# Four granules of layer 0's modulation moved from VectorE's dot products to TensorE

## The chip, the core and the metric

The kernel runs on one core of a Trainium2 chip. The metric is the device time of one execution in microseconds (us). Before the change three runs took 1684.3, 1690.0 and 1689.28 us; their median is 1689.28 us.

## What is computed

A backbone of two layers over 512 tokens (256 context, stream 0, and 256 latent, stream 1), width 1024, float32. Each layer scales, shifts and gates with six vectors per stream that come from a condition vector:

```
mod_l[0..5] = split(silu(c)     @ w_ada[l] + b_ada[l])      # latent stream
mod_c[0..5] = split(silu(c_ctx) @ w_ada[l] + b_ada[l])      # context stream
h = rmsnorm(x, g1) * (1 + mod[1]) + mod[0];  x += mod[2] * mix_heads(h)
h = rmsnorm(x, g2) * (1 + mod[4]) + mod[3];  x += mod[5] * channel_mix(h)
```

`channel_mix` is a dense SwiGLU of width 2816 in layer 0 and a top-2-of-8 expert SwiGLU in layer 1. `w_ada[l]` is 1024 x 6144. The last sixth of its columns, which the change is about, makes mod[5], the gate of the channel mixing. It is first needed when the first down product of the dense SwiGLU is added to x.

## The kernel before

All of x, transposed, stays in SBUF as XT (eight tiles of 128 features x 512 tokens, k = 0 to 7). Weights stream in as granules of 128 x 2048 values (1 MB) through `raw`, a ring of three buffers (five at first); the order of the granules is written out by `stream_plan`, and the sync engine (SP) issues their loads in that order, each as soon as the granule that was in the buffer before has been used. A float32 product is made of three products of rounded parts: ScalarE casts a granule to w_hi (L1127, `upto`), VectorE makes w_lo as the difference (L1633), and TensorE computes hi x hi, hi x lo and lo x hi (`split3`, L448 to L450).

The modulation of layer 0 is made from 24 granules in two ways. Granules 0 to 19 (pairs n = 0 to 9) are `ada` granules: `group` multiplies the padded condition `cpad` (32 columns) with the raw granule on TensorE in plain float32 (L458), two granules for 512 outputs; ScalarE copies the result to `rows` (`save_row`, L1146), TensorE turns it (`turn`, L478: four products with a 128 x 2 result) and VectorE adds the bias into `mod` (`bias_mod`, L1691). Granules 20 to 23 are `dot` granules: VectorE computes each of two halves times two streams as one dot product of 1024 values (`dots`, L1646, and L1653 for the bias), with the condition in `crow`, which the POOL queue loads and ScalarE puts through silu (L1455). The same way is used for layer 1's 24 granules, in later steps of the dense SwiGLU.

The second norm of layer 0 goes as follows. `project_out` makes eight products o 0 to o 7; VectorE adds each to XT (L1999), ScalarE squares it (L1202), VectorE sums the squares (L1745). TensorE sums over partitions (`norm_sum`, L542), ScalarE takes the root (L1210), VectorE the inverse and four diagonal tiles (L1754, L1757), and TensorE spreads them (`norm_spread`, L551). Then VectorE computes t (L1770), ScalarE hT_hi (L1221) and VectorE hT_lo (L1779), for each k and each stream.

`feed_forward` runs over 33 steps, each with one granule: gate/up (two for each of 11 pairs) and down. On TensorE the first gate_up covers steps 0 and 1 together: it takes its granules and four PSUM banks, and then loops over k, waiting for hT_lo of tile k each time. A gate/up step uses banks 0 and 1, or 2 and 3; a down step makes eight products in banks 4, 5 and 6 by turns, and VectorE adds each to XT with the gate of mod (`add_gated`, L1999). Between them ScalarE applies silu (L1465) and casts (L1470), and VectorE multiplies (L2056, `h`) and makes the low part (L2059).

A PSUM bank is given out by `bank(job, b)`: TensorE waits until the last job in that bank has been read, by the count of the reading engine's instruction that is named "read ...". Each engine counts its instructions in its own order, so a wait for a name is a wait for everything that the engine has in front of it. The banks around the second norm are: o 0 0 to o 0 7 in 5, 7, 0, 1, 2, 3, 4, 5; the norm's sums in 6, its spread in 7; the first gate_up in 0, 1, 2, 3.

Of the kernel before, what the change touches and what calls it, by code (L numbers as in the profile page):

```python
# [21 lines left out]
P = 128  # L22
D = 1024
# [60 lines left out]
def dots_ahead():  # L84

    ahead = {2: [(0, 20), (0, 21)], 3: [(0, 22)], 4: [(0, 23)]}
    for i, b in enumerate((5, 7, 8, 10, 11, 13, 14, 16)):
        ahead[b] = [(1, i)]
    for i, b in enumerate((17, 19, 20, 22, 23, 25)):
        ahead[b] = [(1, 8 + 2 * i), (1, 9 + 2 * i)]  # L90
    for i, b in enumerate((26, 28, 29, 31)):
        ahead[b] = [(1, 20 + i)]
    return ahead


def stream_plan():

    plan = [("ada", 0, i) for i in range(2 * BEFORE - 2)]
    for l in range(DEPTH):
# [11 lines left out]
        if l == 0:  # L111
            before = dots_ahead()
            for b in range(3 * FC):
                plan += [("dot",) + x for x in before.get(b, [])]
                plan.append(("ffn", 0, b))
    return plan

# [19 lines left out]
def build(nc, io, table):  # L137
    with ExitStack() as ctx:
# [251 lines left out]
        def source(kind, e, i):  # L390
            if kind == "dot":
                return io["dot"][4 * e + i - (0 if e else 20)]
            return io[kind][e, i]
# [31 lines left out]
        def _(eng):  # L425
# [37 lines left out]
            def plain_group(n, half):  # L463

                if half == 0:
                    eng.wait_ge(act_done, after("cpad"))
                    state["plain"] = bank(f"ada 0 {n}", {9: 6}.get(n))
                group(0, n, half, state["plain"])
# [5 lines left out]
            def turn(l, n):  # L474
                eng.wait_ge(act_done, after(f"row {l} {n}"))
                o = bank(f"modT {l} {n}", 7 if n == 8 else None)
                for j in range(4):
# [350 lines left out]
            def feed_forward():  # L828
# [33 lines left out]
                for b, (kind, s, half) in enumerate(order):  # L862
                    if kind == "gu" and b != 1:
                        gate_up(b, 2 * s + half)
                    elif kind == "d":
                        down(b, s)
# [199 lines left out]
            for l in range(DEPTH):  # L1066
# [14 lines left out]
                attention(l, streams)  # L1081
                project_out(l, streams)
                norm_sum(l, 2, streams)
                if l == 0:
                    norm_spread(l, 2, streams)
                    feed_forward()
                else:
# [23 lines left out]
        def _(eng):  # L1111
# [338 lines left out]
            def feed_forward():  # L1450
                for b, (kind, s, half) in enumerate(order):
                    if b == 0:
                        upto(gindex[("ffn", 0, 1, 0)])
                        eng.wait_ge(*loaded["wide condition"])
# [112 lines left out]
            for l in range(DEPTH):  # L1567
# [18 lines left out]
                deviation(l, 2, streams)  # L1586
                if l == 0:
                    norm(l, 2, streams)
                    feed_forward()
# [27 lines left out]
        def _(eng):  # L1617
# [19 lines left out]
            def dots(g):  # L1637
# [3 lines left out]
                eng.wait_ge(raw_full[place[g]], 16 * use[g])  # L1641
                streams = (0, 1) if l == 0 or i < 8 else (1,)
                for j in range(2):
# [402 lines left out]

            def feed_forward():
                for b, (kind, s, half) in enumerate(order):
                    g = gindex[("ffn", 0, b, 0)]
                    upto(ahead(g, 2 if kind == "gu" else 1))  # L2050
                    if kind == "gu":
# [10 lines left out]
                    else:  # L2062
                        if s == 0:
                            eng.wait_ge(dve_done, after("dots 0 23"))
                        for k in range(KD):
# [419 lines left out]
def lay(inputs):  # L2485
# [6 lines left out]
    io["crow"] = c(np.broadcast_to(np.stack([f("c_ctx"), f("c")[0]]), (P, 2, D)))  # L2492
    io["ada"] = c(f("w_ada")[:1, :, :5120].reshape(1, 2, 4, P, 10, 512).transpose(0, 4, 1, 3, 2, 5).reshape(1, 20, P, GRAN))
    dot = f("w_ada").transpose(0, 2, 1).reshape(DEPTH * 24, 2, P, D).transpose(0, 2, 1, 3).reshape(DEPTH * 24, P, GRAN)
    io["dot"] = c(dot[20:])
    w_in = f("w_in")
# [122 lines left out]
```

## Time and profile before

| | |
|---|---|
| median of three runs | 1689.28 us |
| profiled execution, first to last instruction (span) | 1686.8 us |
| TensorE matmuls busy | 1611.4 us (96%) |
| VectorE busy | 1289.9 us (76%) |
| ScalarE busy | 897.8 us (53%) |
| mean granted TensorE clock | 0.982 of full |

Of the profiled execution only the span is given; the median of the runs stands 2.5 us above it. A busy TensorE is what the kernel is made of: the dense layer (about 317 to 697 us) and the experts (from some 870 us) keep it busy nearly without a break. So the places to read are those where it stands still, and who releases it there. In the rows below a time line gives for each instruction its start, its length, engine and line, operation, result and operands, and in square brackets how long the engine was idle before it and who ended that.

### The profile page before, as it was taken

The page shows a single profiled execution, that of the slowest core. Times are in us where ns is not written, and L with a number is a line of the kernel's source. Part 1 is how long each engine was busy: PE and PEld are TensorE (multiplying, and loading weights), DVE is VectorE, ACT ScalarE, POOL GpSimd, SP SyncE. Part 2 cuts the span into 40 slices and gives each one's busy share as a digit, 9 for nine tenths or more (in the row PEclk, how much of TensorE's full clock was granted, in tenths as well). Part 3 has the DMA queues.
Part 4 walks back from the last instruction along what each step waited for, and adds up shares of the span by engine and source line. Part 5 has one row for each costly group of instructions (what it writes and reads, how often), then busy time and mean ns, then how long its engine had stood idle before and what let it go on. Part 6 is the DMA issues. An engine that isn't in the chain of part 4 may idle for free.

```text
span 1686.8 us, 19520 instructions
## 1 busy us (share of the span) xinstructions
PE 1611.4 (96%) x7452; PEld 1269.6 (75%) x7452; DVE 1289.9 (76%) x1723; ACT 897.8 (53%) x1029; POOL 40.7 (2%) x40
## 2 busy tenths in 40 slices
PE   5999999899999999999899999999999999999996
PEld 2785567778888888786587778888888888888875
DVE  3944473698777865765768998898988889898997
ACT  3324363332222222444657777767777776777764
POOL 1000000000000000000000000000000000000050
PEclk8999999899999999999989999999999999999999
DMA  9225511363455544232147999899989999899982
GB/s 392 86 75 196 222 54 45 131 228 130 170 193 207 203 171 150 74 122 94 43 175 302 361 361 337 348 359 353 359 349 357 346 359 352 342 350 374 366 318 114
DMA packets 55972, 403.43 MB, mean 239 GB/s; under 512 B 6417, under 2 KB 6449, under 8 KB 8769
## 3 DMA queue, kind: packets, MB, share of 16 engines
q1 hardware_dynamic: 53712, 387.47, 60.3%
q0 software_dynamic: 2160, 14.63, 2.3%
q8 instruction: 62, 1.02, 0.2%
q14 instruction: 38, 0.30, 0.1%
HBM read 401.03 MB, written 1.05 MB: 238 GB/s over the span
## 4 chain that ended last, share of the span: by engine, by line
PE 74%; DVE 16%; ACT 5%; issue 3%; DMA 2%; SPq 0%; DVEq 0%; ACTq 0%
PE PS L448 20%; PE PS L450 20%; PE PS L449 20%; DVE w_lo L2272 6%; PE PS L753 2%; DVE w_lo L1633 2%; DMA arena<-in_ada 2%; ACT w_hi L1505 1%; DVE arena L1646 1%; PE PS L1008 1%; DVE XT L1999 1%; PE PS L765 1%; PE PS L778 1%; PE PS L732 1%; PE PS L458 1%
## 5 line engine op out<-in xcount | busy, mean ns | idle before, releaser
L2272 DVE TENSOR_TENSOR w_lo<-arena,w_hi 128x2048 fp32r<-128x2048 f32 (+1 forms) x136 | 305.9, 2254 | 43.3 <-ACT w_hi L1505 43.3
L2272 DVE TENSOR_TENSOR w_lo<-raw,w_hi 128x2048 fp32r<-128x2048 f32 (+1 forms) x133 | 298.9, 2251 | 32.9 <-ACT w_hi L1505 32.4
L1505 ACT CAST w_hi<-arena 128x2048 fp32r<-128x2048 f32 x132 | 251.5, 1909 | 46.2 <-PE PS L450 46.2
L1505 ACT CAST w_hi<-raw 128x2048 fp32r<-128x2048 f32 x129 | 246.9, 1916 | 43.5 <-PE PS L450 43.5
L448 PE MATMUL PS<-hT_hi,w_hi 128*128 128x512 f32 (+1 forms) x576 | 216.1, 375 | 8.6 <-DVE hT_lo L1779 6.9
L449 PE MATMUL PS<-hT_lo,w_hi 128*128 128x512 f32 (+1 forms) x576 | 213.7, 371 | 0.0
L450 PE MATMUL PS<-hT_hi,w_lo 128*128 128x512 f32 (+1 forms) x576 | 213.5, 371 | 0.0
L448 PE MATMUL PS<-w_hi,hT_hi 128*128 128x512 f32 (+1 forms) x448 | 178.5, 398 | 0.9 <-DVE w_lo L1633 0.6
L450 PE MATMUL PS<-w_hi,hT_lo 128*128 128x512 f32 (+1 forms) x448 | 174.6, 390 | 0.0
L449 PE MATMUL PS<-w_lo,hT_hi 128*128 128x512 f32 (+1 forms) x448 | 173.5, 387 | 0.0
L448 PE MATMUL PS<-w_hi,f_hi 128*128 128x512 f32 x352 | 140.4, 399 | 2.1 <-DVE f_lo L2281 2.1
L1633 DVE TENSOR_TENSOR w_lo<-raw,w_hi 128x2048 fp32r<-128x2048 f32 (+1 forms) x54 | 122.3, 2265 | 24.1 <-ACT w_hi L1127 23.9
L449 PE MATMUL PS<-w_lo,f_hi 128*128 128x512 f32 x352 | 139.0, 395 | 0.0
L450 PE MATMUL PS<-w_hi,f_lo 128*128 128x512 f32 x352 | 138.7, 394 | 0.0
L448 PE MATMUL PS<-w_hi,odd_hi 128*128 128x512 f32 x336 | 135.5, 403 | 0.0
L1127 ACT CAST w_hi<-raw 128x2048 fp32r<-128x2048 f32 (+1 forms) x54 | 102.2, 1892 | 60.8 <-PE PS L450 52.1
L448 PEld LDWEIGHTS PS<-hT_hi,w_hi 128*128 128x128 f32 x576 | 109.4, 190 | 30.1 <-DVE hT_lo L1779 7.6
L450 PE MATMUL PS<-w_hi,odd_lo 128*128 128x512 f32 x336 | 131.8, 392 | 0.0
L449 PE MATMUL PS<-w_lo,odd_hi 128*128 128x512 f32 x336 | 131.0, 390 | 0.0
L450 PEld LDWEIGHTS PS<-hT_hi,w_lo 128*128 128x128 f32 x576 | 109.5, 190 | 18.7
L449 PEld LDWEIGHTS PS<-hT_lo,w_hi 128*128 128x128 f32 x576 | 109.6, 190 | 18.3
L1999 DVE SCALAR_TENSOR_TENSOR XT<-PS,mod,XT 128x256 f32<-128x256 f32 x200 | 84.7, 476 | 33.6 <-PE PS L450 33.2
(322 smaller groups left out, 2536.0 us busy)
## 6 DMA issues: line engine op xcount, KB each, us to landing
raw<-in_moe SPq DMA_DIRECT2D x132, 1024.0 KB, 5.2
arena<-in_moe SPq DMA_DIRECT2D x132, 1024.0 KB, 5.2
raw<-in_ffn SPq DMA_DIRECT2D x33, 1024.0 KB, 4.8
raw<-in_dot SPq DMA_DIRECT2D x28, 1024.0 KB, 4.8
raw<-in_ada SPq DMA_DIRECT2D x17, 1024.0 KB, 6.5
raw<-in_out SPq DMA_DIRECT2D x8, 1024.0 KB, 4.9
raw<-in_inb SPq DMA_DIRECT2D x8, 960.0 KB, 4.7
raw<-in_ina SPq DMA_DIRECT2D x5, 1024.0 KB, 5.2
```

The lines of the kernel that those rows point to most:

```text
L448: mm(out, s_hi, m_hi, start=start, stop=False)
L449: mm(out, s_hi, m_lo, start=False, stop=False)
L450: return mm(out, s_lo, m_hi, start=False, stop=stop)
L458: i = mm(o[32 * k:32 * k + 32, :], cpad[:, 4 * half + k, :], w[:, 512 * k:512 * k + 512], start=half == 0, stop=half == 1)
L732: i = mm(o[:, 256 * j:256 * j + 256], wuq[:, k, h, :], cqT[:, k, 256 * s:256 * s + 256], start=k == 0, stop=k == KQ - 1)
L753: i = mm(o[:, q], qT[0:96, n // 2, a:a + P], KT[0:96, h, 0:512 if s else 256], start=True, stop=True)
L765: i = nc.tensor.transpose(o[:, to:to + P], prob[:, u % 4, at:at + P], ident[:, :])
L1127: nc.scalar.copy(w_hi[:, slot[n], 0:w], raw_at(n)[:, 0:w]).then_inc(act_done, 1)
L1505: nc.scalar.copy(w_hi[:, x_slot(j), :], x_raw(n)).then_inc(x_hi, 1)
L1633: v.tensor_tensor(w_lo[:, slot[n], 0:w], raw_at(n)[:, 0:w], w_hi[:, slot[n], 0:w].bitcast(F32), ALU.subtract).then_inc(dve_done, 1)
L1999: v.scalar_tensor_tensor(out=XT[:, k, q], in0=o[:, q], scalar=mod[:, l, j + k, s:s + 1], in1=XT[:, k, q], op0=ALU.mult, op1=ALU.add).then_ ...
L2272: last = v.tensor_tensor(w_lo[:, x_slot(j), q], x_raw(NGR * (i % 2) + j)[:, q], w_hi[:, x_slot(j), q].bitcast(F32), ALU.subtract)
```

## The change

`dots_ahead` loses granules 20 to 23 of layer 0, and `stream_plan` puts them as `ada` granules behind the second dense granule. Pair 10 (granules 20, 21) is multiplied between the last output projection product and the norm's sums, the first half of pair 11 between the sums and the spread, its second half behind the spread and behind the turn of pair 10. Pair 11 is turned behind the first gate_up. ScalarE saves row 10 behind the norm's root and row 11 at the head of the dense layer. VectorE adds the bias of pair 10 at the head of `feed_forward` and that of pair 11 at its step 1.

```diff
 def dots_ahead():
-    ahead = {2: [(0, 20), (0, 21)], 3: [(0, 22)], 4: [(0, 23)]}
+    ahead = {}
...
                 plan.append(("ffn", 0, b))
+                if b == 1:
+                    plan += [("ada", 0, i) for i in range(20, 24)]
...
 @blk.tensor, plain_group and turn
-                    state["plain"] = bank(f"ada 0 {n}", {9: 6}.get(n))
+                    state["plain"] = bank(f"ada 0 {n}", {9: 6, 10: 4, 11: 5}.get(n))
...
-                o = bank(f"modT {l} {n}", 7 if n == 8 else None)
+                o = bank(f"modT {l} {n}", {8: 7, 10: 3, 11: 7}.get(n))
...
 @blk.tensor, feed_forward
                         gate_up(b, 2 * s + half)
+                        if b == 0:
+                            turn(0, 11)
...
 @blk.tensor, the layers
                 project_out(l, streams)
+                if l == 0:
+                    plain(10)
                 norm_sum(l, 2, streams)
                 if l == 0:
+                    plain_group(11, 0)
                     norm_spread(l, 2, streams)
+                    turn(0, 10)
+                    plain_group(11, 1)
                     feed_forward()
...
 @blk.scalar
                     if b == 0:
+                        save_row(0, 11)
...
                 deviation(l, 2, streams)
                 if l == 0:
+                    save_row(0, 10)
                     norm(l, 2, streams)
...
 @blk.vector
-                streams = (0, 1) if l == 0 or i < 8 else (1,)
+                streams = (0, 1) if i < 8 else (1,)
...
             def feed_forward():
+                bias_mod(0, 10)
                 for b, (kind, s, half) in enumerate(order):
                     g = gindex[("ffn", 0, b, 0)]
+                    if b == 1:
+                        bias_mod(0, 11)
                     upto(ahead(g, 2 if kind == "gu" else 1))
...
                         if s == 0:
-                            eng.wait_ge(dve_done, after("dots 0 23"))
+                            eng.wait_ge(dve_done, after("read modT 0 11"))
```

The host lays out all 24 `ada` granules of layer 0, and only layer 1's columns as `dot`.

The order of TensorE's instructions between the output projection and the first gate product, before (L542 the norm's sums, L551 its spread, L448 on hT_hi the gate products):

```order
L450 MATMUL PS<-hT_hi,w_lo 128x512
L542 MATMUL PS<-ones,arena 128x1 [waits dve_done]
L542 MATMUL PS<-ones,arena 128x1 x3
L551 MATMUL PS<-arena,ones 128x128 [waits dve_done] x4
L448 MATMUL PS<-hT_hi,w_hi 128x512 [waits dve_done]
L449 MATMUL PS<-hT_lo,w_hi 128x512
```

and after the change (there L460 is the narrow group, L544 the sums, L553 the spread, L480 the turn, L450 the first of the gate products):

```order
L460 MATMUL PS<-raw,cpad 32x512 [waits raw_full2,dve_done,act_done]
...
L460 MATMUL PS<-raw,cpad 32x512 [waits raw_full0]
...
L544 MATMUL PS<-ones,arena 128x1 [waits dve_done]
...
L460 MATMUL PS<-raw,cpad 32x512 [waits raw_full1,dve_done,act_done]
L460 MATMUL PS<-raw,cpad 32x512 x3
L553 MATMUL PS<-arena,ones 128x128 [waits dve_done] x4
L480 MATMUL PS<-sel,rows 128x2 [waits dve_done,act_done]
L480 MATMUL PS<-sel,rows 128x2 x3
L460 MATMUL PS<-raw,cpad 32x512 [waits raw_full2]
L460 MATMUL PS<-raw,cpad 32x512 x3
L450 MATMUL PS<-hT_hi,w_hi 128x512 [waits dve_done]
```

Pair 10's eight products stand in front of the sums, four of pair 11 in front of the spread, and a turn and four more in front of the gate products.

On VectorE, the end of the second norm and what follows it, before (L1779 the last hT_lo, L1646 and L1653 a dot granule, of which two stand there; L1633 a w_lo, L2056 `h`):

```order
L1779 SCALAR_TENSOR_TENSOR hT_lo<-arena,mod,hT_hi 128x256 [waits dve_done,act_done]
L1779 SCALAR_TENSOR_TENSOR hT_lo<-arena,mod,hT_hi 128x256 [waits dve_done]
L1646 ISA arena,mod<-raw,arena 128x1024 [waits dve_done,raw_full2,act_done]
L1646 ISA mod 128x1
...
L1653 TENSOR_TENSOR mod<-mod,par 128x2 [waits dve_done]
L1653 TENSOR_TENSOR mod<-mod,par 128x2
L1633 TENSOR_TENSOR w_lo<-raw,w_hi 128x2048 [waits act_done]
L2056 TENSOR_TENSOR arena<-PS,arena 128x512 [waits act_done]
L2059 TENSOR_TENSOR h_lo<-arena,h_hi 128x512 [waits act_done]
```

and after the change (L1790 the last hT_lo, L1702 `bias_mod`, L1644 a w_lo, L2070 `h`, L2073 its low part):

```order
L1790 SCALAR_TENSOR_TENSOR hT_lo<-arena,mod,hT_hi 128x256 [waits dve_done,act_done]
L1790 SCALAR_TENSOR_TENSOR hT_lo<-arena,mod,hT_hi 128x256 [waits dve_done]
L1702 TENSOR_TENSOR mod<-PS,par 128x4 [waits pe_done]
L1702 TENSOR_TENSOR mod<-PS,par 128x4
L1644 TENSOR_TENSOR w_lo<-raw,w_hi 128x2048 [waits act_done]
L2070 TENSOR_TENSOR arena<-PS,arena 128x512 [waits act_done]
L2073 TENSOR_TENSOR h_lo<-arena,h_hi 128x512 [waits act_done]
L1702 TENSOR_TENSOR mod<-PS,par 128x4 [waits pe_done]
L1702 TENSOR_TENSOR mod<-PS,par 128x4
```

The two granules of dots are gone from in front of the first w_lo; the bias adds of pair 10 stand behind the norm's last row, those of pair 11 behind the first h.

The loads that SP issues around the change, before:

```order
L2388 DMA raw<-in_out 128x2048 [waits pe_done]
L2388 DMA raw<-in_ffn 128x2048 [waits pe_done]
L2388 DMA raw<-in_ffn 128x2048 [waits dve_done]
L2388 DMA raw<-in_dot 128x2048 [waits dve_done] x2
L2388 DMA raw<-in_ffn 128x2048 [waits dve_done]
L2388 DMA raw<-in_dot 128x2048 [waits dve_done]
L2388 DMA raw<-in_ffn 128x2048 [waits dve_done]
```

and after it:

```order
L2402 DMA raw<-in_out 128x2048 [waits pe_done]
L2402 DMA raw<-in_ffn 128x2048 [waits pe_done]
L2402 DMA raw<-in_ffn 128x2048 [waits dve_done]
L2402 DMA raw<-in_ada 128x2048 [waits dve_done] x3
L2402 DMA raw<-in_ada 128x2048 [waits pe_done]
L2402 DMA raw<-in_ffn 128x2048 [waits pe_done] x3
L2402 DMA raw<-in_dot 128x2048 [waits dve_done]
```

The four granules stand together, and three loads of the dense layer's weights now wait for TensorE, which uses them up, in place of VectorE.

## Rows read from the trace of the kernel before

**Rows 1.** The page, part 1: busy time (share of the span) and instructions.
```profile
PE 1611.4 (96%) x7452; PEld 1269.6 (75%) x7452; DVE 1289.9 (76%) x1723; ACT 897.8 (53%) x1029; POOL 40.7 (2%) x40
```

**Rows 2.** Who TensorE waited for, 300 to 760 us: total, times, longest.
```profile
PE PS L448 <- DVE XT L1999: 4.5, 7, 2.1
```

**Rows 3.** TensorE in time: start, length, line, tiles, count [idle before <-releaser].
```profile
307.01 0.39 PE L449 MATMUL PS<-hT_lo,w_hi 128*128 128x512 f32 x1
307.23 0.39 PE L450 MATMUL PS<-hT_hi,w_lo 128*128 128x512 f32 x1
309.98 1.05 PE L542 MATMUL PS<-ones,arena 128*128 128x1 f32 x8 [2.36 <-DVE arena L1745]
312.01 2.04 PE L551 MATMUL PS<-arena,ones 128*128 128x128 f32 x8 [0.98 <-DVE arena L1757]
316.76 0.77 PE L448 MATMUL PS<-hT_hi,w_hi 128*128 128x512 f32 x1 [2.70 <-DVE hT_lo L1779]
```

**Rows 4.** Time line of VectorE, the norm's tiles.
```profile
314.17 1.66 DVE L1770 SCALAR_TENSOR_TENSOR arena<-XT,gsc,PS 128x256 f32<-128x256 f32 x4 [1.71 <-PE PS L551]
315.74 0.87 DVE L1779 SCALAR_TENSOR_TENSOR hT_lo<-arena,mod,hT_hi 128x256 fp32r<-128x256 f32 x2
...
325.20 1.66 DVE L1779 SCALAR_TENSOR_TENSOR hT_lo<-arena,mod,hT_hi 128x256 fp32r<-128x256 f32 x4
```

**Rows 5.** Windows: us; PE, PEld, DVE, ACT, POOL busy; PEclk, DMA share, GB/s.
```profile
24.00:25.00 1.00, 0.68 (x8) 0.20 (x8) 0.68 (x4) 0.18 (x2) 0.00 (x0) 0.80 1.06 442
311.00:312.00 1.00, 0.04 (x1) 0.02 (x1) 0.60 (x4) 0.26 (x1) 0.00 (x0) 0.66 0.90 377
316.00:317.00 1.00, 0.24 (x1) 0.27 (x2) 1.00 (x4) 0.39 (x1) 0.00 (x0) 0.50 1.11 476
321.00:322.00 1.00, 1.00 (x4) 0.78 (x4) 1.00 (x3) 0.34 (x2) 0.00 (x0) 0.72 0.00 0
```

**Rows 6.** Time line of VectorE, around h 0 and the dots of granule 22.
```profile
341.19 0.68 DVE L2056 TENSOR_TENSOR arena<-PS,arena 128x512 f32<-128x512 f32 x1
...
343.17 1.22 DVE L1646 CUSTOM_DVE_ANT_0 arena<-raw,arena 128x1024 f32<-128x1024 f32 x1
...
348.02 2.28 DVE L1633 TENSOR_TENSOR w_lo<-raw,w_hi 128x2048 fp32r<-128x2048 f32 x1
```

**Rows 7.** Time line of TensorE, its waits in the first dense steps.
```profile
342.02 0.47 PE L448 MATMUL PS<-hT_hi,w_hi 128*128 128x512 f32 x1 [0.98 <-DVE arena L2056]
...
371.17 0.50 PE L448 MATMUL PS<-h_hi,w_hi 128*128 128x512 f32 x1 [2.13 <-DVE XT L1999]
...
374.94 0.50 PE L448 MATMUL PS<-h_hi,w_hi 128*128 128x512 f32 x1 [0.70 <-DVE XT L1999]
```

**Rows 8.** Time line of ScalarE, the first silu.
```profile
339.71 0.60 ACT L1465 ACTIVATE arena<-PS 128x512 f32<-128x512 f32 x1 [8.85 <-PE PS L450]
```

**Rows 9.** Time line of TensorE, a turn between two dense products.
```profile
268.43 0.95 PE L478 MATMUL PS<-sel,rows 128*128 128x2 f32 x8
269.24 0.49 PE L448 MATMUL PS<-hT_hi,w_hi 128*128 128x512 f32 x1
```

**Rows 10.** Time line of TensorE, narrow groups: two at full clock, one at half.
```profile
188.00 1.92 PE L458 MATMUL PS<-raw,cpad 128*32 128x512 f32 x16
...
205.81 1.94 PE L458 MATMUL PS<-raw,cpad 128*32 128x512 f32 x8 [3.55 <-DMA raw<-in_ada]
```

**Rows 11.** Time line of SyncE's queue, the issue for ffn2.
```profile
302.47 0.33 SPq L2388 DMA_DIRECT2D raw<-in_ffn  x1
```

**Rows 12.** The line L1691: ns least/median/most, first and last start.
```profile
L1691 DVE TENSOR_TENSOR mod<-PS,par x20: 148/152/164, 25.3 to 275.9; 128x4 f32<-128x4 f32 x20
```

**Rows 13.** Time line of POOL, the issue of crow.
```profile
308.83 0.53 POOL L2431 DMA_DIRECT2D arena<-in_crow  x1 [152.99 <-DVE XT L1999]
```

**Rows 14.** The DMA view: issues, size of each, median us to landing.
```profile
raw<-in_ada SPq DMA_DIRECT2D x17, 1024.0 KB, 6.5
...
arena<-in_hyc POOLq DMA_DIRECT2D x2, 1920.0 KB, 10.2
```

More of the change, by code:

```diff
@@ L391, in source @@
             if kind == "dot":
-                return io["dot"][4 * e + i - (0 if e else 20)]
+                return io["dot"][i]
             return io[kind][e, i]
@@ L2492, in lay @@
     io["crow"] = c(np.broadcast_to(np.stack([f("c_ctx"), f("c")[0]]), (P, 2, D)))
-    io["ada"] = c(f("w_ada")[:1, :, :5120].reshape(1, 2, 4, P, 10, 512).transpose(0, 4, 1, 3, 2, 5).reshape(1, 20, P, GRAN))
-    dot = f("w_ada").transpose(0, 2, 1).reshape(DEPTH * 24, 2, P, D).transpose(0, 2, 1, 3).reshape(DEPTH * 24, P, GRAN)
-    io["dot"] = c(dot[20:])
+    io["ada"] = c(f("w_ada")[:1].reshape(1, 2, 4, P, 12, 512).transpose(0, 4, 1, 3, 2, 5).reshape(1, 24, P, GRAN))
+    io["dot"] = c(f("w_ada")[1].T.reshape(24, 2, P, D).transpose(0, 2, 1, 3).reshape(24, P, GRAN))
     w_in = f("w_in")
```

## The prediction

> **What bounds the kernel now.** I read the page first: TensorE is busy for 96% of the span [rows 1], so a change counts by what it does to TensorE's few idle places. I then asked who TensorE waited for between 300 and 760 us: VectorE's adds of the down products come first, 4.5 us in seven waits [rows 2]. Third came the time lines of TensorE, VectorE and ScalarE around the second norm and through the first dense steps. The reader is to see three things there. Between the last output projection product and the first gate product TensorE issues only the norm's few products and waits [rows 3], while VectorE computes the normalised tiles from 314.17 to 326.86 (its last row starts at 325.20 and lasts 1.66). TensorE does not wait for all of them: its first gate product starts at 316.76, 0.15 us after the first tile is whole (315.74 + 0.87 = 316.61) [rows 3, 4]. So ten microseconds of VectorE's norm lie beside TensorE's gate products. Last, the clock by windows: granted 1.0 (2.4 GHz) while TensorE was dense, fallen within the slice 311 to 312 after only the norm's products had run, 0.50 (1.2 GHz) when the gate products start, and back at full within the slice 321 to 322 [rows 5].
>
> **What the change takes away.** VectorE loses the dot products of four granules. One granule's take from 343.17 to the next stage at 348.02, 4.85 us with their small adds, so 19 us in all [rows 6]. VectorE is not the bound, so what counts is the TensorE time that waited for it. There are three such places, idle for 0.98, 2.13 and 0.70 us [rows 7]. Products overlap: each lasts 0.39 and the next one starts 0.23 after it [rows 3], so a stall costs 0.16 more than its idle time: 1.14, 2.29 and 0.86. The first is a wait for h 0, which VectorE made only after two granules of dots and one w_lo (341.19, though ScalarE had its silu at 339.71 + 0.60 = 340.31) [rows 6, 8]. The other two are the first down step, where VectorE arrived late with its adds. Without the dots, VectorE has h 0 ready about 0.8 us earlier, and is at the down step in time; so 2.29 + 0.86 = 3.15 us come back there. Of the 1.14 us the moved products of turn(0, 11) now take 0.81 (such a turn between two dense products starts at 268.43 and the next product at 269.24) [rows 9], so 0.33 come back. Together **3.5 us back**.
>
> **What it adds before the norm.** plain(10) is 16 narrow matmul passes, 1.92 us at full clock (188.00) [rows 10]; its two granules were asked for in the places of the first two dot granules, long before. Its bank 4 was read for o 0 6, so it can follow the last product at about 307.5 and end at 309.4, before the norm's sums can start at 309.98: nothing. The first half of granule pair 11 comes behind those sums (309.98 + 1.05 = 311.03) [rows 3] and takes half of 1.92 = 0.96: it ends at 312.0, just where the spread products started. At half clock it takes 1.94 (205.81) [rows 10], and the spread is 0.98 late. Its granule was asked for at 302.47, in the place of ffn2 [rows 11]. Against that, the spread took 2.04 us at half clock; at full it would be 1.02 less. Bounds +1.0 and -1.0; I take **-0.3**, since TensorE now has work from 307.5 to 309.4 and the fall should come somewhat later than 311.3. ScalarE's save of row 10 is one copy, between the norm's root and the first tile that VectorE makes (314.17), and the norm doesn't read it.
>
> **What it adds behind the norm: a bank.** turn(0, 10) writes PSUM bank 3. Bank 3 is read by bias_mod(0, 10) on VectorE, which the change puts at the head of feed_forward, behind the whole norm. But the first gate_up takes four banks, 0 to 3, before its loop over k, and bank(..., 3) makes TensorE wait for "read modT 0 10". So the first gate product no longer waits for the first normalised tile but for all sixteen and the bias adds: 326.86 + 2 x 0.15 (the adds, L1691 before) + the same 0.15 of handover = 327.3 instead of 316.76 [rows 3, 4, 12]. That is **+10.5 us**. Queued behind the waiting product on TensorE are the 96 products of the first two gate steps; every later stage follows TensorE. Nothing hides it: the loop over k was limited by TensorE already (24 us from 316.76 to the stall before 342.02, against 10 that VectorE needs for the tiles), so having all tiles ready saves nothing. The Trainium skill ("PSUM — Partial Sum Buffer", section on PSUM bank collisions) says that the chip doesn't arbitrate between TensorE's write and VectorE's read of a bank, and that semaphores must guard it by bank; it speaks against this change, since by it the wait could not be had for less with this bank. No row of before shows a wait of this kind at this place.
>
> Below that 10.5 us lie the turn (twice 0.95 at half clock, an estimate [rows 9]) and the second half of pair 11 (1.94), done well before 327.3 if its granule has landed by 325.4. It can be asked for only when plain(10) has used the first granule, at about 308.5, while the POOL queue asks for crow, hyc and fw at 308.83 and after; hyc alone took 10.2 us to land [rows 13, 14]. crow (2 x 1024 values a partition, as much as a granule), hyc and this granule are 1.0 + 1.9 + 1.0 MB, with the small fw 4.2 MB, at the 377 GB/s of the slice 311 to 312 [rows 5] 11 us, so about 320; even behind ffn2 and ffn3, 6.3 MB, it would be 326. Hidden, with up to 0.6 us of risk. ScalarE's row 11 and the silu of crow follow at 327 instead of 326; the next weights' cast is wanted by TensorE only at 351.
>
> **The clock.** TensorE starts the gate products at half clock now, and loses about half of 316.76 to 321.5, 2.4 us [rows 5]. After the change it will have stood idle for some ten microseconds before them, so it starts low again: 0, bounds 0 and -2.4. The Trainium skill ("TensorE: Matmul & The Clock Gate", Part 1) has the clock set by how busy TensorE has been lately, by which work put into the gap could keep it at 2.4 GHz. The row that bears on it speaks against: in the slice 24 to 25 it fell while just such narrow groups ran [rows 5]. By the rule the sum would be 2.4 lower, by the row not.
>
> **The sum.** +10.5 (bank 3) - 3.5 (waits gone) - 0.3 (norm earlier) = **+6.7 us** on the profiled execution's 1686.8 us, so a span of 1693.5. The median of the runs before, 1689.28, stands 2.5 above that span; I expect 1696.0, 0.4% slower. A measurement of this kernel tells about 0.5% (8.4 us) from no change, so this would most likely count as no change, on the slow side. Its own range: +5 to +8 from the bounds that I hold likely, with the scatter of the three runs (1684.3 to 1690.0) 1692 to 1699.
>
> **Rivals.**
> 1. *TensorE is not held by bank 3* (the read comes earlier than I think, as if bias_mod ran beside the norm). Then TensorE comes to the gate products behind the turn and the last half group: granule landed at 308.5 + 6.5 to 10.2 = 315 to 318.7 [rows 14], plus 1.94: 317 to 320.6, so 0.2 to 3.9 late in place of 10.5; with 3.8 given back the sum is -3.6 to +0.1, about -2: 1687. For it: the products before the norm cost nothing. Against: the order of VectorE's rows, where the L1702 adds stand behind the last L1790 row. Not slower than before.
> 2. *The first down step's stalls stay*: bank 3 holds TensorE and VectorE still comes late to the adds of down 0, because its step is bound by its own chain (silu, h, cast, h_lo, w_lo of the step ahead) and not by the dots. Then 3.15 is not given back: +9.9, 1699. It decides if VectorE's first add of down 0 ends more than 4.2 us behind TensorE's first down product. Against it: of the ten later down steps, with dots before all of them, TensorE's waits are few and short (of the 4.5 us, five later waits share 1.7) [rows 2, 7].
> 3. *The clock stays up* through the norm, since its gap is broken into by the narrow groups: -2.4 and the norm 1.0 earlier: 10.5 - 3.5 - 1.0 - 2.4 = +3.6, 1693. Against: the wait of ten microseconds comes after the last group.
> That the change doesn't do what it says is excluded by the order of its rows: the four granules are TensorE products there and VectorE's dots are gone.
>
> **How the numbers follow.** Forecast 0.68; rival 1 0.10; rival 2 0.13; rival 3 0.09. The time is the forecast's, 1696.0. The range leaves out most of rival 1 and the edge of rival 2: 1688.5 to 1701. Slower by over 0.5%, above 1697.7: a quarter of the forecast's (0.17) and nearly all of rival 2 (0.12), 0.29. Faster by over 0.5% only as the tail of rival 1 and of the scatter: 0.03. Within 0.5%: 0.68.
>
> **What would show it.** In the changed profile TensorE's first gate product should be released by VectorE's L1702 (mod) and not by L1790 (hT_lo), some 16 us behind the last output projection product's end in place of 9, with VectorE's norm rows at the same times or up to 1 us earlier. The gate products should start at a granted clock of 0.5. VectorE's busy time should fall by 19 us, and down 0 should show no wait for L1999's adds. Wrong would be: a gate product that starts beside the norm (rival 1), waits of 2 us in down 0 (rival 2), a clock of 1.0 at the first gate product (rival 3), or a wait for raw<-in_ada that ends behind the norm.

## The result, and the profile after the change

The changed kernel took 1694.49 us (median of seven runs, 1692.55 to 1697.25) beside 1689.41 us of the kernel before on the same chip (seven runs, 1683.91 to 1690.0): a ratio of 1.0039, 95% interval 1.0027 to 1.0051. So it is 5 us slower, which is inside the 0.5% that the prediction called no change, and 1.5 us below the predicted 1696.0. Its profiled execution took 1692.55 us, with a span of 1690.6.

What VectorE did is gone, as the busy times say (before: [rows 1]); TensorE has 48 more products, VectorE 18.5 us less:

```profile
PE 1613.9 (95%) x7500; PEld 1271.8 (75%) x7500; DVE 1271.4 (75%) x1687; ACT 898.5 (53%) x1031; POOL 40.7 (2%) x40
```

Who TensorE waited for between 300 and 760 us: one new wait that was not there before, and VectorE's adds down from 4.5 to 1.7 us [rows 2]. (The lines have moved by a few: L448 of before is L450 here, L1999 is L2010, L1779 is L1790.)

```profile
PE PS L450 <- DVE mod L1702: 11.4, 1, 11.4
...
PE PS L450 <- DVE XT L2010: 1.7, 5, 0.3
```

TensorE in time around the second norm, to be read beside [rows 3]: narrow groups ahead of the sums, half a pair behind them, the spread, the turn, the other half, and then nothing until the gate products. Their releaser is the bias add of L1702, not the normalised tile of L1790.

```profile
304.50 1.92 PE L460 MATMUL PS<-raw,cpad 128*32 128x512 f32 x16
306.93 1.05 PE L544 MATMUL PS<-ones,arena 128*128 128x1 f32 x8 [0.51 <-DVE arena L1756]
307.91 1.07 PE L460 MATMUL PS<-raw,cpad 128*32 128x512 f32 x8
308.96 1.13 PE L553 MATMUL PS<-arena,ones 128*128 128x128 f32 x8
309.93 0.95 PE L480 MATMUL PS<-sel,rows 128*128 128x2 f32 x8
310.81 1.07 PE L460 MATMUL PS<-raw,cpad 128*32 128x512 f32 x8
323.28 0.76 PE L450 MATMUL PS<-hT_hi,w_hi 128*128 128x512 f32 x1 [11.40 <-DVE mod L1702]
```

VectorE in the same stretch (before: [rows 4]): the first low tile starts at 311.77 and the last ends at 322.89; the bias adds follow, and 0.25 us behind them TensorE starts.

```profile
311.77 0.88 DVE L1790 SCALAR_TENSOR_TENSOR hT_lo<-arena,mod,hT_hi 128x256 fp32r<-128x256 f32 x2
...
321.22 1.67 DVE L1790 SCALAR_TENSOR_TENSOR hT_lo<-arena,mod,hT_hi 128x256 fp32r<-128x256 f32 x4
322.81 0.22 DVE L1702 TENSOR_TENSOR mod<-PS,par 128x4 f32<-128x4 f32 x2
```

The clock in windows (before: [rows 5]; PEclk is the value behind the busy times): full through the narrow groups and for 2 us behind the last of them, then 0.50 from 314 on and through the first 4.4 us of gate products (before: the first 4.8).

```profile
313.00:314.00 1.00, 0.00 (x0) 0.00 (x0) 1.00 (x4) 0.91 (x2) 0.00 (x0) 1.00 1.00 425
314.00:315.00 1.00, 0.00 (x0) 0.00 (x0) 1.00 (x4) 0.35 (x1) 0.00 (x0) 0.50 1.29 546
...
326.00:327.00 1.00, 1.00 (x4) 0.81 (x3) 0.00 (x0) 1.00 (x1) 0.00 (x0) 0.50 0.00 0
327.00:328.00 1.00, 1.00 (x5) 0.78 (x4) 0.64 (x1) 0.33 (x1) 0.00 (x0) 0.68 0.00 0
```

And at h 0 the wait of [rows 7] is replaced by the moved turn:

```profile
347.20 0.95 PE L480 MATMUL PS<-sel,rows 128*128 128x2 f32 x8
348.01 0.49 PE L450 MATMUL PS<-hT_hi,w_hi 128*128 128x512 f32 x1
```

**How the two traces are laid side by side.** The norm's sums start 3.05 us earlier in the profile after (306.93 against 309.98). The work ahead of it is the same, and in both the sums stand 2.36 us behind the last output projection product (before: [rows 3]); in the eight further profiles below the same row starts anywhere from 306.76 to 310.24. Two profiles of one and the same kernel, bank4, have it at 308.43 and 309.59. So I take the shift for scatter from the first 300 us and none of the change's. I therefore count from the start of these sums. In the table, "gate" is the first gate product; "down 0" a narrow 33 x 256 product of the filter just ahead of the first down step's adds, "filter 2" the next one of it (64 x 64), behind these adds and two more gate steps, just ahead of the second down step, "layer 1" the sums of layer 1's first norm. All are starts of TensorE rows, in us behind the sums. Each ratio is to runs of the kernel before that were made beside it (their medians are 1687.94 to 1689.41 us), so kernels are better compared by the ratio than by the median.

| kernel | sums at | gate | down 0 | filter 2 | layer 1 | median, us | ratio to before (95%) |
|---|---|---|---|---|---|---|---|
| before | 309.98 | 6.78 | 54.01 | 91.14 | 388.52 | 1689.41 | |
| after | 306.93 | 16.35 | 63.08 | 96.85 | 394.30 | 1694.49 | 1.0039 (1.0027, 1.0051) |
| bank4 | 308.43 | 5.86 | 50.55 | 84.30 | 381.74 | 1683.29 | 0.9973 (0.9963, 0.9983) |
| read_mid | 308.06 | 9.26 | 55.24 | 89.02 | 386.42 | 1686.48 | 0.9991 (0.9982, 0.9999) |
| bank4_dots | 309.73 | 5.86 | 54.43 | 89.73 | 387.22 | 1689.15 | 1.0008 (0.9998, 1.0017) |
| before_filler | 306.76 | 5.86 | 54.58 | 90.20 | 387.62 | 1687.37 | 0.9991 (0.9983, 1.0000) |
| before_no_dots | 310.09 | 6.78 | 53.47 | 87.21 | 384.61 | 1683.28 | 0.9968 (0.9958, 0.9977) |
| bank4_again | 309.59 | 5.86 | 50.52 | 84.28 | 381.71 | 1683.91 | 0.9959 (0.9944, 0.9974) |
| bank4_spread | 310.24 | 5.86 | 50.55 | 84.29 | 400.53 | 1701.13 | 1.0066 (1.0051, 1.0081) |
| bank4_no18 | 309.95 | 5.86 | 50.55 | 84.30 | 381.69 | 1681.32 | 0.9951 (0.9935, 0.9968) |

Of after against before: the gate products are 9.57 later, 9.07 at down 0, 5.71 at filter 2, and 5.78 at layer 1. Behind layer 1's mixing the gap of these two profiles is 6.6, and at the end 6.85. That part also scatters: from the start of layer 1 to the end, the ten profiles of the table take 987.0 to 991.4 us on unchanged code. The spans themselves differ by 3.8, which is 6.85 less the 3.05 of the earlier start.

### The profile page after: what moved, and what is told of

It is laid out like the page before. It is cut to its first block, busy times and chain, and to the rows that moved or that the text cites. A ratio compares the mean times of both kernels' runs of the same rounds, so it can differ in the third digit from the quotient of the medians.

```text
span 1690.6 us, 19584 instructions
## 1 busy us (share of the span) xinstructions
PE 1613.9 (95%) x7500; PEld 1271.8 (75%) x7500; DVE 1271.4 (75%) x1687; ACT 898.5 (53%) x1031; POOL 40.7 (2%) x40
## 4 chain that ended last, share of the span: by engine, by line
PE 78%; DVE 13%; ACT 4%; issue 2%; DMA 1%; SPq 0%; DVEq 0%; ACTq 0%
PE PS L450 21%; PE PS L452 21%; PE PS L451 21%; DVE w_lo L2286 6%; PE PS L755 2%; ACT w_hi L1515 1%; PE PS L1012 1%; DVE w_lo L1644 1%; PE PS L734 1%; PE PS L780 1%; PE PS L460 1%; PE PS L767 1%; DVE XT L2010 1%; DMA arena<-in_ada 1%; PE PS L638 1%
## 5 line engine op out<-in xcount | busy, mean ns | idle before, releaser
L450 PE MATMUL PS<-hT_hi,w_hi 128*128 128x512 f32 (+1 forms) x576 | 217.0, 377 | 16.1 <-DVE mod L1702 11.4
L450 PE MATMUL PS<-w_hi,hT_hi 128*128 128x512 f32 (+1 forms) x448 | 178.5, 398 | 1.0 <-DVE w_lo L1644 0.6
L1644 DVE TENSOR_TENSOR w_lo<-raw,w_hi 128x2048 fp32r<-128x2048 f32 (+1 forms) x54 | 122.4, 2267 | 30.5 <-ACT w_hi L1136 30.4
L450 PE MATMUL PS<-w_hi,f_hi 128*128 128x512 f32 x352 | 140.4, 399 | 2.1 <-DVE f_lo L2295 2.1
L450 PEld LDWEIGHTS PS<-hT_hi,w_hi 128*128 128x128 f32 x576 | 110.3, 191 | 37.8 <-DVE mod L1702 12.3
L450 PE MATMUL PS<-w_hi,odd_hi 128*128 128x512 f32 x336 | 135.6, 403 | 0.0
L2010 DVE SCALAR_TENSOR_TENSOR XT<-PS,mod,XT 128x256 f32<-128x256 f32 x200 | 84.8, 477 | 35.2 <-PE PS L452 34.6
```

The costliest lines, as they stand in the source:

```text
L450: mm(out, s_hi, m_hi, start=start, stop=False)
L1644: v.tensor_tensor(w_lo[:, slot[n], 0:w], raw_at(n)[:, 0:w], w_hi[:, slot[n], 0:w].bitcast(F32), ALU.subtract).then_inc(dve_done, 1)
L2010: v.scalar_tensor_tensor(out=XT[:, k, q], in0=o[:, q], scalar=mod[:, l, j + k, s:s + 1], in1=XT[:, k, q], op0=ALU.mult, op1=ALU.add).then_ ...
```

## The experiments

Theory: the whole loss is TensorE's wait for the reader of bank 3, and the gain is VectorE's missing dots. Rival: without that wait TensorE would still be late, held by the turn, the groups or their granules; or the dots' absence gives nothing.

**bank4.** The change with another bank for the turn, one whose reader TensorE needs only later:

```
-                o = bank(f"modT {l} {n}", {8: 7, 10: 3, 11: 7}.get(n))
+                o = bank(f"modT {l} {n}", {8: 7, 10: 4, 11: 7}.get(n))
```

> The changed kernel with one number other: turn(0, 10) writes bank 4 in place of bank 3, so that the first gate products need no bank that VectorE reads behind the norm. Theory (the bank wait costs 10.5 us and hides a good clock): the first gate product starts 5.5 to 6.5 us behind the start of the norm's sums in place of 16.35 (323.28 - 306.93 in the changed kernel's trace), released by hT_lo of tile 0 and no longer by the bias adds. In the changed kernel the clock fell at 314.0, 7 us behind the sums, so the gate products now start at full clock: 10.5 less for the wait and up to 2.4 less for the clock: 1694.5 - 10.5 - (0 to 2.4) = 1681.6 to 1684, ratio to before 0.9955 to 0.997. Rival (the narrow groups or the landing of the last granule hold TensorE as well): the first gate product waits for raw<-in_ada or stands behind the narrow groups, up to 4 us later, 1686 to 1688. Rival (the bank has no part in it): 1694, no change.

Measured: 1683.29 us, ratio 0.9973 (0.9963 to 0.9983), faster than before by 5.0 us. TensorE's first gate product waits 0.92 us, for the first low tile:

```profile
312.31 1.06 PE L460 MATMUL PS<-raw,cpad 128*32 128x512 f32 x8
314.29 0.47 PE L450 MATMUL PS<-hT_hi,w_hi 128*128 128x512 f32 x1 [0.92 <-DVE hT_lo L1790]
```

It stands at +5.86, which is 10.49 less than the +16.35 of after. And in the windows from 304 to 331 the clock never falls:

```profile
313.00:314.00 1.00, 0.37 (x4) 0.00 (x0) 1.00 (x3) 0.92 (x3) 0.00 (x0) 1.00 0.95 401
314.00:315.00 1.00, 0.71 (x3) 0.65 (x4) 1.00 (x4) 0.43 (x2) 0.00 (x0) 1.00 0.97 410
315.00:316.00 1.00, 1.00 (x6) 0.78 (x6) 1.00 (x3) 0.48 (x2) 0.00 (x0) 1.00 1.09 462
```

From the gate products to down 0 after takes 46.73 us and bank4 44.69: 2.04 us is what the half clock costs there. So one number in the table of banks is worth 10.49 + 2.04 = 12.5 us locally, and 11.2 between the medians of the two kernels.

**read_mid.** Bank 3 stays, but its read stands ahead of tile 4 of the norm instead of behind tile 7:

```
+                    if l == 0 and w == 2 and n == 4:
+                        bias_mod(0, 10)
...
             def feed_forward():
-                bias_mod(0, 10)
```

> The changed kernel with bank 3 kept, but VectorE's bias adds of pair 10 put into the norm, before tile 4 of t, instead of behind it. Theory (TensorE is released by that read wherever it stands): the first gate product starts about 0.4 us behind hT_lo of tile 2 (315.7 in the changed kernel's trace), so at 316.1 in place of 323.28: 7.2 us less, and at half clock or just above it as the clock had fallen at 314.0: 1687.3, ratio to before about 0.9988. Rival (TensorE waits for all tiles for another reason, such as hT itself): 1694.5, no change.

Measured: 1686.48 us, ratio 0.9991 (0.9982 to 0.9999). The wait is for the same row and 7.1 us shorter, since VectorE comes to it earlier:

```profile
317.32 0.77 PE L450 MATMUL PS<-hT_hi,w_hi 128*128 128x512 f32 x1 [4.31 <-DVE mod L1702]
```

Gate at +9.26, in between. The length of the wait follows the place of the read in VectorE's order, which is the bank theory in a second setting. The clock fell here too, but only in the slice 316 to 317:

```profile
313.00:314.00 1.00, 0.00 (x1) 0.00 (x0) 1.00 (x3) 0.55 (x2) 0.00 (x0) 1.00 0.95 401
316.00:317.00 1.00, 0.00 (x0) 0.00 (x0) 1.00 (x6) 0.68 (x2) 0.00 (x0) 0.85 1.04 442
317.00:318.00 1.00, 0.68 (x2) 0.62 (x3) 1.00 (x4) 0.51 (x2) 0.00 (x0) 0.50 0.97 416
```

**before_no_dots.** The other half of the change by itself: the kernel before, its four granules loaded but not multiplied (two copies stand for each; layer 0's last gate is not the reference's).

```
             def dots(n):
+                if l == 0:
+                    v.tensor_copy(mod[:, l, 2 * i:2 * i + 2, 0], raw_at(g)[:, 0:2])
+                    ...
+                    return
```

> The kernel before, with the loads of the four dot granules kept but the 16 dot products and their bias adds left out (two copies of 128 x 2 values take their place, so layer 0's last gate isn't the reference's); no narrow groups on TensorE. With the kernel before, the one with idle groups and the one with bank 4 it fills a square: groups or none, dots or none. Seen so far, from the start of the norm's sums to the product of 64 x 256 after the second down step: 91.1 us before, 90.2 with the groups alone, 84.3 with groups and without dots. Theory (VectorE's dots hide what the clock gains): without dots and without groups the first gate products run at half clock as before, the waits for h 0 and in down 0 (1.14 + 3.15) are gone: 86.8, 4.3 us less than before, so 1684.0 where before stands at 1688.3, ratio 0.9975, and the groups are then worth 2.5 us more. Rival (the gains are of the dots alone and the clock counts for nothing): 84.3 as with bank 4, ratio 0.996.

Measured: 1683.28 us, ratio 0.9968 (0.9958 to 0.9977). The gate products start at +6.78 and at half clock as before; of the wait for h 0 only 0.14 us is left, the long waits of the first down step are gone, and filter 2 is 3.93 us earlier, at 87.21 where the theory had 86.8 and the rival 84.3. The waits of 300 to 760 us keep the 1.7 us of the later steps:

```profile
PE PS L448 <- DVE hT_lo L1785: 3.6, 2, 2.7
PE PS L448 <- DVE XT L2005: 1.7, 5, 0.3
```

**bank4_dots.** bank4 with the same sixteen dot products put back on VectorE, on data that no one needs:

```
+                    if plan[n] in (("ffn", 0, 2), ("ffn", 0, 3), ("ffn", 0, 4)):
+                        for r in range(2 if plan[n][2] == 2 else 1):
+                            idle_dots()
```

> As the kernel with bank 4, and VectorE makes 16 dot products of the same shape as the removed ones, at the places where they stood (two granules' worth before the third w_lo, one each before the fourth and fifth), with crow in place of the weights and the sums thrown away; no loads are added. Theory (what came back in the first down step came from the dots): the waits of about 2.1 and 0.7 us in down 0 return, and h 0 is late behind the turn: 3.2 to 4 us slower than the kernel with bank 4, so 1685 to 1688. Rival (the waits went for another reason, as the order of the loads): the same time as the kernel with bank 4.

Measured: 1689.15 us, ratio 1.0008 (0.9998 to 1.0017): all of bank4's gain is gone, 5.9 us between the medians and 5.43 at filter 2, where 3.2 to 4 were expected. The expectation was too small, and the trace says why:

```profile
340.60 0.47 PE L450 MATMUL PS<-hT_hi,w_hi 128*128 128x512 f32 x1 [2.22 <-DVE arena L2083]
...
369.54 0.50 PE L450 MATMUL PS<-h_hi,w_hi 128*128 128x512 f32 x1 [0.34 <-DVE XT L2023]
...
373.31 0.50 PE L450 MATMUL PS<-h_hi,w_hi 128*128 128x512 f32 x1 [0.70 <-DVE XT L2023]
```

TensorE, early by its clock, waits 2.22 us for h 0 where it waited 0.98 before [rows 7]; and behind this wait the clock falls:

```profile
341.00:342.00 1.00, 1.00 (x6) 0.82 (x5) 0.84 (x3) 1.00 (x2) 0.00 (x0) 0.90 0.61 180
342.00:343.00 1.00, 1.00 (x4) 0.81 (x3) 0.95 (x1) 1.00 (x2) 0.00 (x0) 0.50 1.00 426
343.00:344.00 1.00, 1.00 (x4) 0.71 (x4) 1.00 (x3) 0.40 (x1) 0.00 (x0) 0.50 0.82 344
...
345.00:346.00 1.00, 1.00 (x6) 0.79 (x5) 1.00 (x3) 0.00 (x0) 0.00 (x0) 0.90 0.00 0
```

At down 0 it is 3.88 us behind bank4: 2.22 + 0.16 of wait, and 1.5 that I put down to the half clock.

**before_filler.** The kernel before with useless products in the places of the change's (`filler`: the same narrow groups, without a granule; `filler_turn`: the turn, with no reader), so nothing is changed but what TensorE does in the gap:

```
+                if l == 0:
+                    filler("filler 10", 4, True)
+                    filler("filler 10", 4, False)
                 norm_sum(l, 2, streams)
                 if l == 0:
+                    filler("filler 11", 5, True)
                     norm_spread(l, 2, streams)
+                    filler_turn()
+                    filler("filler 11", 5, False)
```

> The kernel before with useless narrow products on TensorE at the places of the changed kernel (16 before the norm's sums, 8 before the spread, a turn of 8 and 8 more behind it), from cpad and rows, into banks 4, 5 and 3 that nobody reads; VectorE's dots stay. Tells apart what TensorE's clock gains from the groups. Theory (they keep the clock at 2.4 GHz): the spread is 1 us shorter, the norm begins 0.9 earlier, and the first gate products run at full clock, 2.4 less: 1689.4 - 3.3 = 1686.1, ratio 0.998. Rival (the clock falls all the same, or the gate product stands behind the groups): 1688.5 to 1690.5.

Measured: 1687.37 us, ratio 0.9991 (0.9983 to 1.0000). The theory (1686.1) and its rival (1688.5 to 1690.5) both miss, and both have a part of it. The gate products do start at full clock and 0.92 us earlier, since the spread takes 1.13 us at full clock and 2.04 at half; then TensorE comes to h 0 too early:

```profile
308.79 1.13 PE L563 MATMUL PS<-arena,ones 128*128 128x128 f32 x8
...
312.62 0.47 PE L448 MATMUL PS<-hT_hi,w_hi 128*128 128x512 f32 x1 [0.92 <-DVE hT_lo L1797]
...
337.88 0.76 PE L448 MATMUL PS<-hT_hi,w_hi 128*128 128x512 f32 x1 [3.21 <-DVE arena L2074]
```

The wait has grown from 0.98 to 3.21 us: from the first gate product to the first product behind this wait it is 25.26 us in both kernels, so the full clock won nothing there. The product behind the wait lasts 0.76, at half clock, which stays until 341:

```profile
338.00:339.00 1.00, 1.00 (x3) 0.81 (x4) 0.59 (x1) 0.38 (x1) 0.00 (x0) 0.50 1.10 418
...
340.00:341.00 1.00, 1.00 (x4) 0.71 (x3) 1.00 (x3) 1.00 (x1) 0.00 (x0) 0.50 0.96 401
341.00:342.00 1.00, 1.00 (x6) 0.82 (x5) 1.00 (x3) 0.83 (x2) 0.00 (x0) 0.96 0.45 188
```

So with the dots in place, the clock that is won at 312 is lost again at 338. The four corners at filter 2 are 91.14 (before), 90.20 (narrow products alone), 87.21 (dots gone alone) and 84.30 (both, bank4). The narrow products are worth 0.94 us with the dots there and 2.91 without them; the dots cost 3.93 at half clock and 5.90 at full. The two parts of the change are worth more together than apart: 6.84 against 4.87. The corners are not quite alike, since bank4 also has turn(0, 11) between the gate products and its groups use real granules; bank4_dots, which differs from bank4 by the dots alone, gives 5.43 for them at full clock in place of 5.90.

**bank4_again and bank4_spread.** What remains in bank4 are five waits of 0.35 us for VectorE's adds, one in every three steps from 536 to 671 us, where steps with two dot granules of layer 1 stand. I took these for the cause, and spread the granules one to a step:

```
-    for i, b in enumerate((5, 7, 8, 10, 11, 13, 14, 16)):
+    for i, b in enumerate((2, 3, 5, 7, 8, 10, 11, 13)):
         ahead[b] = [(1, i)]
-    for i, b in enumerate((17, 19, 20, 22, 23, 25)):
-        ahead[b] = [(1, 8 + 2 * i), (1, 9 + 2 * i)]
-    for i, b in enumerate((26, 28, 29, 31)):
-        ahead[b] = [(1, 20 + i)]
+    for i in range(16):
+        ahead[16 + i] = ahead.get(16 + i, []) + [(1, 8 + i)]
```

> The kernel of the run bank4 once more, as the partner of bank4_spread on the same chip. It should repeat 1683.3 us within 1 us, and its five waits of 0.35 us at the down steps that have double dots of layer 1 beside them (536.27 to 670.57).

> bank4 with the 24 granules of layer 1's modulation that are still dot products on VectorE spread one to a step (eight of them from step 2 on instead of step 5 on, the other sixteen at steps 16 to 31), where bank4 has two of them in each of six steps. Theory (TensorE's remaining waits in the dense steps come from VectorE being late at steps with double dots): the five waits of 0.35 us vanish, each with the 0.16 us of overlap 0.51, so 2.5 us less than bank4: 1680.8. Rival (VectorE's load is only moved: steps 2 and 3, the ones before the first down step, now have a granule of dots of 4.85 us, and bring back waits for h 0 or in the first down step, 1.1 to 3.4 us in the trace of the kernel before): 1682 to 1684, the same as bank4.

Measured: bank4_again 1683.91 us, as bank4. bank4_spread 1701.13 us, ratio 1.0066 (1.0051 to 1.0081): 17 us slower than bank4_again, and both ideas were wrong, the rival too, for steps 2 and 3 cost nothing (filter 2 at 84.29). The loss lies in five waits of 2.2 to 3.0 us, one in every three steps:

```profile
PE PS L448 <- DVE XT L2008: 14.1, 6, 3.0
```

One of them, on TensorE and on VectorE:

```profile
577.41 0.40 PE L450 MATMUL PS<-h_hi,w_lo 128*128 128x512 f32 x1
580.64 0.50 PE L448 MATMUL PS<-h_hi,w_hi 128*128 128x512 f32 x1 [2.83 <-DVE XT L2008]
```

```profile
573.46 1.65 DVE L2008 SCALAR_TENSOR_TENSOR XT<-PS,mod,XT 128x256 f32<-128x256 f32 x4
575.03 1.21 DVE L1655 CUSTOM_DVE_ANT_0 arena<-raw,arena 128x1024 f32<-128x1024 f32 x1
...
577.51 2.29 DVE L1642 TENSOR_TENSOR w_lo<-raw,w_hi 128x2048 fp32r<-128x2048 f32 x1
579.71 2.44 DVE L2008 SCALAR_TENSOR_TENSOR XT<-PS,mod,XT 128x256 f32<-128x256 f32 x6
```

In a down step VectorE makes two adds, then the work ahead (the dots, if the stream has any there, and w_lo), then the other adds; TensorE has only three banks for the down products and waits for the third add. Work that the stream puts ahead of the granule of step 18, 21, 24, 27 or 30 lands exactly between these adds. The table of before skips just these steps. And behind this wait the clock falls: 0.70 in the slice 581 to 582, 0.50 in 582 to 584, 1.00 again in 585 to 586. So it does behind four of the five waits, but not behind the first, of 2.24 us. That fits the lengths: three steps take 33.6 us in bank4, 36.1 from the first wait's end to the second's, which is 2.5 more of waiting, and 37.6 from the second's to the third's, which is 2.5 more of waiting and 1.5 of half clock.

```profile
581.00:582.00 1.00, 1.00 (x5) 0.80 (x4) 1.00 (x3) 0.00 (x0) 0.00 (x0) 0.70 0.95 401
582.00:583.00 1.00, 1.00 (x4) 0.81 (x3) 0.17 (x2) 0.00 (x0) 0.00 (x0) 0.50 0.97 410
```

The first wait, and the clock behind it:

```profile
506.94 0.50 PE L448 MATMUL PS<-h_hi,w_hi 128*128 128x512 f32 x1 [2.24 <-DVE XT L2008]
```

```profile
507.00:508.00 1.00, 1.00 (x5) 0.82 (x6) 1.00 (x4) 0.00 (x0) 0.00 (x0) 1.00 1.01 426
```

**bank4_no18.** To tell the place from the amount, the same stream with these five granules one step earlier:

```
     for i in range(16):
-        ahead[16 + i] = ahead.get(16 + i, []) + [(1, 8 + i)]
+        b = 16 + i - (i % 3 == 2)
+        ahead[b] = ahead.get(b, []) + [(1, 8 + i)]
```

> bank4_spread with the dot granules of steps 18, 21, 24, 27 and 30 (the second gate step of a pair, just ahead of a down step) each put one step earlier, so that steps 17, 20, 23, 26 and 29 have two. The number of granules in every three steps is that of bank4_spread. Theory formed from the trace of bank4_spread (a granule of dots in the step just ahead of a down step stands between VectorE's last adds and the next ones, so TensorE waits 2.2 to 3.0 us for XT, and the clock falls to 0.5 for 3 us behind each of these waits): the five long waits shrink to the 0.35 us that bank4 has, and the time returns to bank4's: 1683 to 1685. Rival (it is the amount of VectorE's work in these steps, or the transfers of the granules pulled forward, that holds TensorE): at least half of the 17 us stays, 1692 to 1701.

Measured: 1681.32 us, ratio 0.9951 (0.9935 to 0.9968). The same granules in every three steps, and the 19 us are back (layer 1 at 381.69 against 400.53). It was the place. The five short waits are still there, 0.35 each:

```profile
571.34 0.50 PE L449 MATMUL PS<-h_hi,w_hi 128*128 128x512 f32 x1 [0.35 <-DVE XT L2009]
```

The last of them (672.06) has no double dots beside it, so these waits are not the double dots'. w_lo alone (2.28 us) stands between VectorE's adds there; whether moving it would free them was not tried. bank4_no18 and bank4 can't be told apart: their ratios overlap and the table has them at the same places.

## Why the prediction was right

**The bank, +10.5: right in mechanism and size.** The profile shows the row that the prediction named: a gate product released by L1702. By bank4, which changes nothing else, the wait costs 10.49 us. read_mid shows that its length is the place of the read in VectorE's order. Rival 1 (not held by bank 3; 1687) is refuted, and its price was too high besides: it let TensorE wait for the last granule until 315 to 318.7, but the second half of pair 11 starts at 310.81 without a wait. The forecast had the same transfer wrong: it let the granule land at about 320, behind crow, hyc and fw. It was issued at 305.62 and landed 4.9 us later, at 313.6 in the times of before. Behind the wait for the bank this cost nothing either way. Two sentences of the prediction do not hold. The wait could be had for less with this bank: read_mid keeps bank 3 and its guard, and waits 4.31 us. And "some 16 us behind the last output projection product's end in place of 9" mixes two starting points: 16.35 is counted from the norm's sums, where before has 6.78; from that product's end it is 18.7 us in place of 9.1, near the 19.3 that +10.5 and -0.3 give.

**The norm, -0.3 with bounds of ±1.0: the mis-sized term.** It measured -0.92, at the edge of the bounds. The step that failed is the clock in the gap: I let the fall come "somewhat later than 311.3", after the row of slice 24 to 25, where the clock fell amid narrow groups [rows 5]. In the gap it did not fall amid them: it stayed 1.00 until 314, 2 us behind the last of them, and so the half group took 1.07 and the spread 1.13 us in place of 2.04. What sets the two apart is not shown. In the slice at 24 TensorE waited for a granule (it is busy for 0.68), while from 308 to 312 the groups, the spread and the turn are back to back; but in the four slices ahead of 24 it was busy all the time too, and the clock fell all the same:

```profile
23.00:24.00 1.00, 1.00 (x12) 0.41 (x11) 0.00 (x0) 0.57 (x2) 0.00 (x0) 1.00 0.97 401
```

The rule of the Trainium skill ("TensorE: Matmul & The Clock Gate", Part 1), that the clock is set by how busy TensorE has been lately, agrees with the gap of the norm; the fall at 24 does not follow from it. I had let that one row decide.

**The dots' waits, -3.5: right.** Behind the gate products 0.50 comes back by down 0 (0.33 predicted; the half clock is 0.4 us shorter there, which would be another 0.2, an estimate) and 3.36 in the first down step (3.15 predicted), 3.86 in all. before_no_dots gives 3.93 for the dots alone, without the turn. Rival 2 (the stalls of down 0 stay; 1699) is refuted: none is in the trace of after, and they vanish with the dots alone.

**The clock at the gate products, 0: right.** They start at 0.50 after the long wait, as the prediction had it. Rival 3 (1693: the clock stays up through the norm) took half of what it said: the norm was 0.9 earlier, and the wait behind the last group ended it. Its -2.4 was real as soon as the wait was gone: 2.04 in bank4. The time alone could not have told it from the forecast, since 1694.49 lies 1.5 us from both 1693 and 1696.0; the 0.50 at the gate products does.

**The sum.** +10.49 - 0.92 - 3.86 = +5.71 us at filter 2, against +6.7 predicted; the medians differ by 5.1. The profiled spans differ by 3.8, since the start of the one was 3.05 us quicker, which the prediction's scatter covered and its terms did not. The range of 1688.5 to 1701 also holds the 1689.4 of the kernel before, so that the time fell into it says little; what carries the account is the row of L1702 and bank4.

**What I did not see**, since the terms were added one by one, is that the clock and the dots depend on each other. In this kernel VectorE's lateness sets a time that TensorE can't pass; what TensorE wins in the clock before it becomes a longer wait, and the waits of 2.22 and 3.21 us that came of it were followed by half clock.

## What to carry to other kernels

When a small product is slipped into a gap, ask of its PSUM bank who takes it next and where its reader's read stands in that engine's order; the cost is everything queued ahead of the read, here 10.5 us for a read of 0.15. Choose the bank by that, not by whether it is free when written. Deferrable work on an engine that feeds another belongs behind the row that is waited for: the same dots cost 0 or 19 us by one step's difference.

## What the runs showed of the hardware

- With narrow float32 groups (128 x 32 weights) between the norm's products, back to back, the granted clock stayed at 1.00 for the whole gap of the norm in bank4 and before_filler, and until the wait behind the last group in read_mid (in the slice 316 to 317) and after (314). The kernel before, with only the norm's products in the gap, was at 0.66 and then 0.50 [rows 5]. In the slice 24 to 25 of [rows 5] it fell behind such groups all the same.
- The same wait, 2 to 3 us long, did or didn't cost clock. One of 2.13 at 371.17 [rows 7] and one of 2.24 (bank4_spread, 506.94) left it at 1.00; one of 2.22 (bank4_dots), ones of 2.83 and 3.03 (bank4_spread) and one of 3.21 (before_filler) were followed by some 3 us at 0.50. Where it happened, the wait was worth about 1.5 us more than its idle time. The length alone does not decide it, as 2.22 and 2.24 show; what does was not tried.

The row of before for that wait, 371 to 373:

```profile
371.00:372.00 1.00, 0.83 (x4) 0.69 (x5) 1.00 (x4) 0.41 (x1) 0.00 (x0) 1.00 1.00 426
372.00:373.00 1.00, 1.00 (x6) 0.82 (x5) 1.00 (x1) 0.00 (x0) 0.00 (x0) 1.00 0.51 213
```

- The narrow groups at full clock take 1.07 us for eight passes alone and 1.92 for sixteen together; at half clock eight take 1.94 [rows 10].
